# Both up projections in groups of 512 gate and 512 value columns, each of the seven products 512 moving columns wide in a PSUM bank of its own

## What is computed

```python
# first block
h2 = rmsnorm(x, norm_ffn[l])
u = h2 @ w_up[l]                                   # 256 x 2048 by 2048 x 11264
u = up[:, :-2] * cw[0] + up[:, 1:-1] * cw[1] + up[:, 2:] * cw[2] + conv_b[l]   # up: u padded along tokens
gate, val = jnp.split(u, 2, axis=-1)
x = x + (jax.nn.silu(gate) * val) @ w_down[l]
# second block
a, b = jnp.split(h @ w_in, 2, axis=-1)             # w_in here: w_ffn_in, the same shape
return (jax.nn.silu(a) * b) @ w_out
```

## Time and profile before

| | |
|---|---|
| median of 3 runs | 2770.83 us (2769.65 to 2771.43) |
| the profiled execution, time | 2769.89 us |
| its span | 2768.1 us |
| TensorE's granted clock | 0.999 |
| busy: TensorE products, weight loads | 2747.4 us, 2407.5 us |
| busy: VectorE, ScalarE, GpSimd | 2216.1, 518.0, 338.4 us |
| read from HBM | 565.49 MB, 206 GB/s over the span |

### The profile page before, as it was taken

The page is one execution under the profiler, slowest core; times in us unless marked ns, Lnnn a source line. Parts: engine busy times, 40 slices in busy tenths (PEclk is TensorE's granted clock), DMA queues, the critical chain, the costliest instruction groups (busy, mean ns, idle before and its releaser), DMA issues.

```text
span 2768.1 us, 35449 instructions
## 1 busy us (share of the span) xinstructions
PE 2747.4 (99%) x13412; PEld 2407.5 (87%) x13412; DVE 2216.1 (80%) x3363; ACT 518.0 (19%) x1065; POOL 338.4 (12%) x462
## 2 busy tenths in 40 slices
PE   9999999999999999999999999999999999999998
PEld 8888888888888888888888888888888888888887
DVE  7888888999999999997776567876788888766554
ACT  3221122001443444430002122211200000000000
POOL 1011221001112111120101002200011111000000
PEclk9999999999999999999999999999999999999999
DMA  8777666677666666668775555555566666555553
GB/s 273 242 257 231 215 212 218 230 241 230 212 216 216 221 220 219 218 220 283 269 252 169 152 156 142 160 165 173 172 218 208 222 217 204 173 174 190 175 175 122
DMA packets 276380, 571.80 MB, mean 207 GB/s; under 512 B 25370, under 2 KB 26778, under 8 KB 275696
## 3 DMA queue, kind: packets, MB, share of 16 engines
q1 hardware_dynamic: 244528, 460.18, 51.5%
q0 software_dynamic: 31248, 109.01, 12.2%
q10 hardware_dynamic: 432, 0.34, 0.0%
HBM read 565.49 MB, written 3.93 MB: 206 GB/s over the span
## 4 chain that ended last, share of the span: by engine, by line
PE 77%; issue 16%; DVE 4%; DVEq 2%; POOLq 0%; POOL 0%; DMA 0%; ACT 0%; ACTq 0%
PE PS L560 72%; DVEq L1078 2%; DVE sums L1079 1%; DVE sums L1081 1%; PE PS L696 0%; PE PS L727 0%; DVE ring L1070 0%; PE PS L570 0%; PE PS L603 0%; DVEq L1096 0%; DVE sums L1069 0%; DVE x_tok L1708 0%; DVE mem L1103 0%; PE PS L980 0%; PE PS L881 0%
## 5 line engine op out<-in xcount | busy, mean ns | idle before, releaser
L560 PE MATMUL PS<-sums,mem 128*128 128x256 f32 x4056 | 1206.3, 379 | 0.0
L560 PE MATMUL PS<-ring,mem 128*128 128x256 f32 x3788 | 1070.9, 379 | 0.0
L560 PEld LDWEIGHTS PS<-sums,mem 128*128 128x128 f32 x4056 | 770.6, 190 | 104.8
L560 PE MATMUL PS<-ring,act_t 128*128 128x256 f32 x3076 | 833.0, 379 | 0.1
L560 PEld LDWEIGHTS PS<-ring,mem 128*128 128x128 f32 x3788 | 715.7, 190 | 97.5 <-issue 1.6
L560 PEld LDWEIGHTS PS<-ring,act_t 128*128 128x128 f32 x3076 | 581.6, 190 | 80.4 <-issue 2.2
L1069 DVE TENSOR_TENSOR sums<-ring 128x512 f32<-128x512 f32 x431 | 303.3, 704 | 303.7 <-PE PS L560 273.5
L1079 DVE TENSOR_TENSOR sums<-sums,ring 128x512 f32<-128x512 f32 x431 | 306.7, 712 | 33.3 <-issue 0.9
L1081 DVE TENSOR_TENSOR sums<-sums,ring 128x512 f32<-128x512 f32 x431 | 305.4, 709 | 33.8 <-issue 2.1
L1187 DVE SCALAR_TENSOR_TENSOR mem<-mem,small 128x1024 f32<-128x1024 f32 x240 | 308.4, 1305 | 28.6 <-DMA mem<-in_w_mod 10.9
L560 PE MATMUL PS<-sums,act_t 128*128 128x256 f32 x1092 | 324.8, 379 | 0.0
(11 more groups left out here) (277 smaller groups left out, 1286.8 us busy)
## 6 DMA issues: line engine op xcount, KB each, us to landing
ring<-in_w_in SPq DMA_DIRECT2D x240, 512.0 KB, 3.7
mem<-in_w_mod POOLq DMA_DIRECT2D x192, 512.0 KB, 4.8
ring<-in_w_up SPq DMA_DIRECT2D x176, 512.0 KB, 3.7
ring<-in_w_ffn_in SPq DMA_DIRECT2D x176, 512.0 KB, 3.5
ring<-in_w_down SPq DMA_DIRECT2D x88, 512.0 KB, 4.6
ring<-in_w_ffn_out SPq DMA_DIRECT2D x88, 512.0 KB, 4.5
ring<-in_w_out SPq DMA_DIRECT2D x64, 512.0 KB, 3.8
ring<-in_w_branch_a SPq DMA_DIRECT2D x16, 512.0 KB, 4.0
```

What stands on the lines that cost most here:

```text
L560: mm = pe.matmul(product(g, j), of(j, 2 * (c if part is None else part) + q), weights(j, n, q), start=lead and j in OPENS, stop=tail, skip ...
```

## The change

The stages "up" and "up2" become 11 groups of 8 chunks instead of 22 of 4. A chunk there is now 2 tiles of contraction by 1024 columns, 512 of the gate and the same 512 of the value: half 0 of the ring's slot holds the gate's columns, half 1 the value's. The two columns of blocks of the seven-product scheme are gate and value, each 512 wide, so a chunk is 7 products of 512 moving columns, and a group is seven whole banks, 0 to 6. Only one such group fits, so the next one follows in the same banks. The gather is one for gate and value, at the last chunk of the group, and what came behind the two gathers comes behind the one. Ahead of up2 the norm's tiles are turned and combined one by one (in banks 5, 6 and then 7), since a chunk needs only two tiles of contraction. The bodies of the gather and of the four additions stay, with 512 columns in a run where there were two runs of 256. Eight loads and pieces of the modulation move from the gate and branch stages to down: by stage, the pieces are proj 25, gate 20 (24 before), branch 8 (12), wout 15, up 44, down 48 (40), up2 32. In the diff `up_turn`, the loop behind it and the `mod_loads` are those of the first up projection (VectorE, GpSimd); the products in parts are TensorE's at the start of up2.

```diff
+            if WIDE[g]:
+                bank = (3, 0, 1, 2, 4, 5, 6)[j]
+                return PSF[:, CN * bank:CN * (bank + n)]
...
+            def load_wide(n, w, kt, cols):
+                for q in range(2):
+                    if n >= SLOTS:
+                        sp.wait_ge(s["weight_used"], 2 * (n - SLOTS) + q + 1)
+                    sp.dma_start(ring[:, n % SLOTS, q, :, :], w[:, kt:kt + 2, cols[q]:cols[q] + CN])\
...
             def product_free(g, j):
...
+                if WIDE[g]:
+                    freed = {Q2: 1, Q7: 2, Q5: 3, Q3: 4} if WIDE[before] else {Q2: 0, Q5: 1, Q3: 3, Q4: 4}
+                elif WIDE[before]:
+                    freed = {Q2: 3, Q7: 4, Q3: 4} if SIDE[g] else {Q2: 1, Q7: 1, Q3: 2}
...
+            def wide_products(n, g, c, of, kinds):
+                b11, b12, b21, b22 = wide_weights(n)
+                weight = {Q1: b11, Q2: b21, Q3: b22, Q7: b12, Q5: wide_sum(n, 0), Q6: wide_sum(n, 1),
+                          Q4: wide_sum(n, 2)}
+                lead, tail = c == 0, c == 7
+                for j in kinds:
+                    if lead:
+                        product_free(g, j)
+                    mm = pe.matmul(product(g, j), of(j, c), weight[j], start=lead, stop=tail, skip_group_check=True)
+                    if tail and j in (Q1, Q6, Q5):
+                        mm.then_inc(s["acc_done"], 1)
+                    if j in (Q2, Q4):
+                        mm.then_inc(s["weight_used"], 1)
+
+            def wide_chunk(n, g, c, of):
+                pe.wait_ge(s["sums_ready"], n + 1)
+                wide_products(n, g, c, of, (Q1, Q2, Q6, Q7, Q5, Q3, Q4))
...
+            def up_turn(i, j):
                 if j == 0:
+                    turn_blocks(up_g, 2 * i)
                 if j == 1:
                     turn_blocks(up_v, 2 * i + 1)
+                if j == 2:
                     conv_sides(up_g4, hidden[:, 4 * i:4 * i + 4, :], i, "up_g_based", 0)
                 if j == VALUE_SIDES:
                     conv_sides(up_v4, conv_v, i, "up_v_based", KF)
...
                     if i:
-                        up_value(i - 1, j)
-                    if j == 4:
+                        up_turn(i - 1, j)
+                    if j == 7:
                         if i:
                             ve.wait_ge(s["up_g_act"], i)
-                        gather(G0["up"] + 2 * i, up_g)
-                    if j == 5:
-                        turn_blocks(up_g, 2 * i)
+                            ve.wait_ge(s["hidden_done"], i)
+                        gather_wide(G0["up"] + i, up_g, up_v)
                     mod_halves(n)
...
-                        norm_pieces("ffn2", 0, 2, ffn2_tmp)
+                        norm_piece("ffn2", 0, ffn2_tmp)
                         weights_in(pe, n)
...
+                        wide_products(n, g, j, of_f2, (Q1, Q2))
+                        norm_piece("ffn2", 1, ffn2_tmp)
...
+                        wide_products(n, g, j, of_f2, (Q6, Q7, Q5, Q3))
+                        pe.wait_ge(norm_sems["ffn2"]["kept"], 2)
+                        wide_products(n, g, j, of_f2, (Q4,))
...
-    for _j in range(1, 4):
+    for _j in range(1, 4 if _k % 2 else 3):
-for _k in range(16):
-    if _k % 4 != 2:
+for _k in range(1, 16, 2):
-    for _j in (1, 2, 5, 6):
+    for _j in (0 if _k else 1, 3, 5, 6):
-    HALVES[N0["down"] + _k] = 2 if _k in (24, 30) else 1
+    HALVES[N0["down"] + _k] = 2 if _k in (21, 22, 28, 29, 30, 31, 32, 39, 40, 41) else 1
...
                     pool.tensor_tensor(h4, h4, up_v4, MUL).then_inc(s["hidden_done"], 1)
+                    mod_loads(1)
                     pool.drain()
                     combine(*pairs_of(i - 1), "forms_h")
-                mod_loads(2)
+                    mod_loads(1)
+                else:
+                    mod_loads(2)
```

More of the change, by code:

```diff
@@ L42 @@
 STAGES = [("proj", 9, 4, "two"), ("gate", 8, 4, "one"), ("branch", 8, 2, "two"), ("wout", 4, 4, "two"),
-          ("up", 22, 4, "two"), ("down", 4, 11, "two"), ("ctx", 3, 4, "one"), ("mix", 10, 4, "one"),
-          ("wout2", 4, 4, "two"), ("up2", 22, 4, "two"), ("down2", 4, 11, "two")]
+          ("up", 11, 8, "wide"), ("down", 4, 11, "two"), ("ctx", 3, 4, "one"), ("mix", 10, 4, "one"),
+          ("wout2", 4, 4, "two"), ("up2", 11, 8, "wide"), ("down2", 4, 11, "two")]
 N0, G0 = {}, {}
-SIDE, BEFORE, FINAL = [], [], []
+SIDE, BEFORE, FINAL, WIDE, WIDE_CHUNKS = [], [], [], [], set()
 _n = 0
@@ L52 @@
         _side = _k % 2 if _banks == "two" else 0
-        BEFORE.append(max((_g for _g in range(len(SIDE)) if SIDE[_g] == _side), default=None))
+        BEFORE.append(max((_g for _g in range(len(SIDE)) if SIDE[_g] == _side or WIDE[_g]), default=None))
         SIDE.append(_side)
+        WIDE.append(_banks == "wide")
         FINAL.append(_n + (_k + 1) * _chunks - 1)
+    if _banks == "wide":
+        WIDE_CHUNKS.update(range(_n, _n + _groups * _chunks))
     _n += _groups * _chunks
 CHUNKS = _n
+for _g in range(1, len(SIDE)):
+    assert not WIDE[_g] or WIDE[_g - 1] or SIDE[_g - 1] == 1
 Q1, Q2, Q6, Q7, Q5, Q3, Q4 = range(7)
@@ L121 @@
         BANK7.append(("ctx", _p - 36))
+    _p = _n - N0["up2"]
+    if 1 <= _p < 7:
+        BANK7.append(("ffn2", _p + 1))
     THROUGH7.append(len(BANK7))
@@ L548, in product_free @@
                     pe.wait_ge(s["first_kept"], g)
-                before = BEFORE[g]
-                if before is not None and j in (Q2, Q7, Q3):
-                    pe.wait_ge(s["acc_free"], 4 * before + {Q2: 1, Q7: 3, Q3: 4}[j])
+                before = g - 1 if WIDE[g] else BEFORE[g]
+                if before is None:
+                    return
+                if WIDE[g]:
[3 more added lines that the diff above has]
+                else:
+                    freed = {Q2: 1, Q7: 3, Q3: 4}
+                if j in freed:
+                    pe.wait_ge(s["acc_free"], 4 * before + freed[j])
             def chunk(n, g, c, chunks, of, part=None):
@@ L1758, in _ @@
                 norm_tok("ffn2", x_tok, ffn2_tmp, j)
-            norm_combine("ffn2", 0, ext_f2, "forms_ffn2")
-            x_add_piece(2)
-            ve.drain()
-            for j in (4, 5):
-                norm_tok("ffn2", x_tok, ffn2_tmp, j)
-            x_add_piece(3)
-            norm_combine("ffn2", 1, ext_f2, "forms_ffn2")
+            ffn2_forms(1)
             def up2_value(i):
-                gather(G0["up2"] + 2 * i + 1, up2_v)
                 ve.wait_ge(s["up_g_act"], 12 + i)
@@ L1789, in _ @@
                     if i == 0 and j < 2:
[L1790 removed]
+                        x_add_piece(2 + j)
+                        ve.drain()
+                        for k in (4 + 2 * j, 5 + 2 * j)[:2 - j]:
+                            norm_tok("ffn2", x_tok, ffn2_tmp, k)
+                    if (i, j) == (0, 2):
+                        norm_tok("ffn2", x_tok, ffn2_tmp, 7)
+                    if i == 0 and j < 6:
+                        ffn2_forms(j + 2)
                     if i and j == 0:
                         up2_value(i - 1)
[L1793 to L1799 removed]
+                    if i and 1 <= j <= 4:
+                        hidden_turn(i - 1, j - 1)
+                    if j == 7:
+                        gather_wide(G0["up2"] + i, up2_g, up2_v)
                     mod_halves(n)
@@ L2061, in _ @@
                         first_keep(G0["down"] + g)
-                    if g == 0:
-                        up_value(10, c)
+                    if g == 0 and c == 0:
+                        up_turn(10)
                     if g == 3 and c >= 3:
```

177 lines of the change are left out of this document (96 added, 81 removed).

## The result

The changed kernel takes 2773.68 us (median of 20 runs, 2771.59 to 2777.29), the kernel before 2769.59 us (20 runs, 2768.84 to 2771.43). The ratio is 1.0014, with a 95% interval of 1.0008 to 1.0020: 4 us slower, which is inside the 0.2% that I called no change, 12.9 us from the forecast of 2760.8 and above the whole range. The forecast was taken off a median of 3 runs, 2770.83; over 20 runs the kernel before lies 1.2 us lower, so its 10.0 us of gain would have meant 2759.6. The span is 2772.2 us and the granted clock 0.998 on the mean.

What follows compares the result with a forecast made beforehand. TensorE, busy 99% of the span, was taken as the bound, with VectorE nearly full in up. Records 6.2, waits 3.5 and up2's start 0.3 sum to 10.0 us gained: 2760.8 us forecast, range 2757.5 to 2767.5.

Steps and rivals of the forecast that it cites:

- The records: TensorE in up and up2: each 512-column record saves 2.5 ns over two of 256; 2464 records, 6.2 us (3.7 to 8.6).
- Rival (c): TensorE's records in up and up2 save nothing, running at twice 215.9 ns: 2767.0 us; chance 0.05.
- The moved pieces: Modulation pieces moved from gate and branch to down: 3.5 us gained (0 to 3.5), the extra work in down hidden.
- Both waits: TensorE's waits for `merged` at wout's start, 2.1 us, and `x_tok` at up's start, 1.4 us, should go.
- The start of up2: First two chunks and transposes of up2: 0.3 us gained, between 1 us lost and 1 us gained.
- VectorE's load in a block of up: VectorE keeps 1.1 us spare per block and could start the gather 2.9 us earlier than needed, so nothing is lost.
- The step's sum: VectorE's work added up per block of up: 46.5 us of 48.1, against 47.4 of 48.4 before.
- the combine: GpSimd's work beside VectorE's additions in up: one 0.69 us addition takes 1.22, in all 1.2 us more per block.
- (a): VectorE late to the gather, stalling TensorE at up to 22 group ends; at 1 us each 2783 us; chance 0.08.
- (b): VectorE late to the gather in up alone: 11 ends x 0.6 = 6.6 us, 2767.4 us; chance 0.11.
- (d): Short waits at group ends drop TensorE's clock to 1.2 GHz: 22 slow chunks, 132 us, 2893 us; chance 0.02.

Runs made afterwards that it cites:

- experiment 1: Changed kernel with GpSimd's product of gate and value in the first up projection cut to one column (output not the model's): 2760.79 us, ratio 0.9967.
- experiment 5: Changed kernel with the product of gate and value in the first up projection done by VectorE, behind the value's sides, instead of GpSimd: 2764.37 us, ratio 0.9983.
- experiment 10: Changed kernel with product on VectorE, last up piece behind the gather, later gate store, and down's first four double pieces at chunks 1, 3, 5, 6: 2757.99 us.
- experiment 11: Kernel of experiment 10 with down's ten two-piece chunks at every second chunk from 22 to 40, not in rows: 2758.34 us, ratio 0.9958.
- experiment 4: Changed kernel with wide groups in up2 alone; up as before the change, the eight moved pieces kept: 2764.98 us, ratio 0.9982.
- experiment 2: Kernel before with only the eight moved pieces and loads of the modulation: 2768.34 us, ratio 0.9993.
- experiment 3: Changed kernel with the eight moved pieces and loads back in gate and branch, wide groups kept: 2776.24 us, ratio 1.0022.
- experiment 8: Kernel before with the value's convolution sides at chunk 3 instead of 4, nothing else: 2778.38 us, ratio 1.0031.
- experiment 7: Changed kernel with product on VectorE, last up piece behind the gather, and the second gate vector's store behind down2's fourth load: 2764.25 us, ratio 0.9979.
- experiment 6: Changed kernel with the last modulation piece of each up block at chunk 7 behind the gather, not chunk 6; product still on GpSimd: 2769.62 us, ratio 0.9997.
- experiment 9: Wide groups in up2 alone, moved pieces kept, with the second gate vector's store behind down2's fourth load: 2763.39 us, ratio 0.9977.

## Why the prediction was wrong, point by point

**The records: right.** 429.2 ns against the 429.3 reckoned, 3.1 us in each stage. Rival (c) is out.

**The moved pieces: right in wout, not hidden in down.** Both waits went as reckoned. That down's double pieces are "hidden" did not hold in every kernel: by the waits lists, experiments 1, 5, 10 and 11 have no late addition there, experiment 4 has 0.8 us of them, the changed kernel 1.6 and experiment 2 has 2.8. That a backlog of VectorE from up decides this is my reading; experiment 10 fits it, experiment 2 was not looked into. Alone the moved pieces are worth 1.9 us by the medians, and the interval reaches from 4.4 gained to 0.6 lost.

**The start of up2: right**, -0.6 us against -0.3, inside the 1 us either way.

**The step that failed: VectorE's load in a block of up.** The prediction said that GpSimd's product "needs the value's sides at E + 30.3", set only its deadline, and costed it "at nothing". The Trainium skill (SBUF - State Buffer, "Who interferes with whom"), which I cited, says that an operation with two SBUF inputs contends with a GpSimd instruction that reads SBUF. The trace agrees: 2.0 us on an addition at every product. The same section of the Trainium skill says of VectorE's two-port modes that the one that issues first has the shared ports for its whole instruction and the other is blocked. Read that way, the rows above fit within 0.2 us: the product of 838.77 would have waited for the two additions under way (to 839.82), then run its 2.36 us to 842.02, and the addition of 839.90 would have done its 0.69 us behind it. That is my reading, and no run separates it from another. I applied the rule to the combine, which the trace of before showed beside additions, and to the gather, but not to the product, which in before was seen only beside the gather. The step's sum, 46.5 of 48.1 us, lacks 2.0 us in ten blocks and the reductions' 2.4 us in three: 48.5 and 50.9 of 48.1, so that VectorE falls behind by 0.4 us in a block and by 2.8 in one with reductions. Experiment 1 takes the product away and gives 2760.8, the forecast's number, though that is partly luck: its last gather of up2 is 2.0 us late, against 1.4 us more than reckoned gained for `merged` and `x_tok` (3.5 + 1.4 against 3.5), of which 1.2 are the slow first stretch of the profiled execution before.

**The rivals.** What happened is (a)'s mechanism at (b)'s size in up, 6.1 us at the block ends where (b) had 6.6, with additions that (b) did not have: 3.2 us at the hand-over to down, because lateness adds up over blocks and the last one has the reductions; 1.7 us of clock; and 1.0 at the end of up2 for a store that I had not looked at. (d) came true in small, once, behind a wait of 2.45 us; the wait of 3.2 us at 1198 was not followed by a lower clock, nor were two of 2.43 and 2.51 us in experiment 3. The Trainium skill (TensorE: Matmul & The Clock Gate, "A second HAM failure mode: psum-queue depth-cycling") puts the lowering down to small idles of TensorE between groups. In the changed kernel the clock stayed at 1.00 behind the block ends with waits of 1.7 us (806) and 0.7 us (953), so only the one long wait bears the rule out; in experiment 1, 1204 records follow each other over seven banks without an idle, and this does not test it.

**What stays open:** Why VectorE waits up to 6 us for a piece's load in down was not measured by itself; spreading the double pieces shortens the waits (experiment 11), which fits with load on the transfers and does not prove it. That the clock fell behind some waits and not behind others of the same length is unexplained.

## What to carry to other kernels

When a step is moved, look not only at when its result is due but at what will run beside it: here GpSimd's product cost nothing beside operations with one input from PSUM and 2 us beside additions with two SBUF inputs, and the engine that is nearest to full pays for it. Moving the job to the crowded engine was cheaper (1.22 us) than letting the other engine block it. Reckon an engine's load by block with the rare jobs in it, since a lead of two chunks hides an average but the block with the extra job sets the wait; and when a wait goes, look at where the backlog comes due, as from the gathers to the start of down here.

## What the runs showed of the hardware

- A VectorE addition of 512 elements, both inputs in SBUF, ended half a microsecond behind GpSimd's product of 1024 elements (0.69 us grew to 2.68), while the product itself took 3.26 us instead of 2.36. The addition that began 0.37 us after the product kept its 0.68 (839.14, and 1035.80 in experiment 8).
- TensorE's granted clock went to 0.50 to 0.51, its lower level, for some 3.4 us behind waits of 2.45 us (up, 1002 us) and 3.3 us (experiment 7, 1232 us), for some 5.7 us behind the wait of 5.7 us of experiment 6, and not at all behind one of 3.2 us (1198 us) or two of 2.43 and 2.51 us (experiment 3, 908 and 1106 us). A wait of TensorE can thus cost 1.7 to 3 us more than its length, and need not.
- A store of 2048 single words on SyncE's queue stood ahead of the loads that VectorE then waited 8.3 us for (experiment 1). When the store was moved four loads on, VectorE's wait moved with it (9.6 us at 2478.5 in experiment 4, 8.4 us at 2503.3 in experiment 9).
